# Two feed-forward blocks of a decoder trunk: gate and up by seven half-size block products in place of eight

## The reference, cut to what matters

```python
def rmsnorm(x, g):
    y = x * lax.rsqrt(jnp.mean(x * x, axis=-1, keepdims=True) + EPS)
    return y * g

def swiglu_ffn(h, w_gu, w_down):
    g, u = jnp.split(h @ w_gu, 2, axis=-1)
    return (jax.nn.silu(g) * u) @ w_down

def reference(x, mem, ...):            # x (1, 512, 1024), all float32
    for i in range(2):
        x = x + 0.5 * swiglu_ffn(rmsnorm(x, n_ffn1[i]), ffn1_w_gu[i], ffn1_w_down[i])
        x = x + mixer(rmsnorm(x, n_mix[i]))           # i = 0: gated linear attention, i = 1: pooling
        x = x + mem_cross_attn(rmsnorm(x, n_xattn[i]), rmsnorm(mem, n_mem[i]), ...)
        x = x + 0.5 * swiglu_ffn(rmsnorm(x, n_ffn2[i]), ffn2_w_gu[i], ffn2_w_down[i])
    return rmsnorm(x, n_final)
```

## Time and profile before

| | |
|---|---|
| median of 3 runs | 1993.26 us (1993.07 to 1993.73) |
| span of the profiled execution | 1992.3 us |
| PE busy | 1983.5 us (100%) |
| DVE busy | 930.9 us (47%) |
| ACT busy | 710.2 us (36%) |
| POOL busy | 160.8 us (8%) |
| mean granted TensorE clock | 0.999 of 2.4 GHz |

### The profile page before, as it was taken

The page is one execution under the profiler, slowest core; times in us unless marked ns, Lnnn a source line. Parts: engine busy times, 40 slices in busy tenths (PEclk is TensorE's granted clock), DMA queues, the critical chain, the costliest instruction groups (busy, mean ns, idle before and its releaser), DMA issues.

```text
span 1992.3 us, 23096 instructions
## 1 busy us (share of the span) xinstructions
PE 1983.5 (100%) x9182; PEld 1654.4 (83%) x9182; DVE 930.9 (47%) x1007; ACT 710.2 (36%) x865; POOL 160.8 (8%) x201
## 2 busy tenths in 40 slices
PE   9999999999999999999999999999999999999998
PEld 7888888888898888888888888888898888888887
DVE  5343443487865654434343443433287544434323
ACT  5222232256554543222222322222156443322222
POOL 2000001100112120000001000000112022200000
PEclk9999999999999999999999999999999999999999
DMA  5323352323434533232223323222353324432221
GB/s 176 105 88 102 100 142 76 104 64 106 129 126 127 169 106 106 84 105 88 96 95 100 106 84 105 87 98 95 121 165 114 103 85 127 158 105 96 94 95 74
DMA packets 204153, 214.53 MB, mean 108 GB/s; under 512 B 21970, under 2 KB 186960, under 8 KB 204096
## 3 DMA queue, kind: packets, MB, share of 16 engines
q1 hardware_dynamic: 180416, 192.95, 29.6%
q0 software_dynamic: 6432, 17.64, 3.4%
q10 hardware_dynamic: 17248, 3.16, 0.9%
HBM read 203.23 MB, written 10.49 MB: 107 GB/s over the span
## 4 chain that ended last, share of the span: by engine, by line
PE 96%; DVE 1%; DMA 1%; ACT 1%; issue 1%; SPq 0%; ACTq 0%; POOL 0%; DVEq 0%
PE ps L368 32%; PE ps L369 32%; PE ps L370 32%; DMA p_scratch<-sq 0%; ACT w_hi L1198 0%; DVE w_lo L1731 0%; DMA raw<-in_ffn_w_gu 0%; DVE sums L2213 0%; DMA p_tok<-p_scratch 0%; DVE sums L2233 0%; SPq L390 0%; DVE up L2411 0%; SPq L418 0%; PE ps L943 0%; PE ps L1138 0%
## 5 line engine op out<-in xcount | busy, mean ns | idle before, releaser
L368 PE MATMUL ps<-h_hi,w_hi 128*128 128x512 f32 (+1 forms) x1728 | 667.3, 386 | 0.2 <-DVE h_lo L1734 0.2
L369 PE MATMUL ps<-h_lo,w_hi 128*128 128x512 f32 (+1 forms) x1728 | 665.8, 385 | 0.0
L370 PE MATMUL ps<-h_hi,w_lo 128*128 128x512 f32 (+1 forms) x1728 | 665.8, 385 | 0.0
L1731 DVE TENSOR_TENSOR w_lo<-raw,w_hi 128x2048 fp32r<-128x2048 f32 (+4 forms) x195 | 417.4, 2141 | 461.8 <-ACT w_hi L1198 461.8
L1198 ACT ACTIVATE w_hi<-raw 128x2048 fp32r<-128x2048 f32 (+4 forms) x195 | 347.6, 1783 | 271.0 <-PE ps L370 266.9
L368 PEld LDWEIGHTS ps<-h_hi,w_hi 128*128 128x128 f32 x1728 | 324.7, 188 | 65.8 <-DVE h_lo L1734 0.9
L370 PEld LDWEIGHTS ps<-h_hi,w_lo 128*128 128x128 f32 x1728 | 324.6, 188 | 64.8
L369 PEld LDWEIGHTS ps<-h_lo,w_hi 128*128 128x128 f32 x1728 | 324.7, 188 | 64.0
L368 PE MATMUL ps<-mid_hi,w_hi 128*128 128x512 f32 x528 | 205.6, 389 | 0.0
L370 PE MATMUL ps<-mid_hi,w_lo 128*128 128x512 f32 x528 | 205.5, 389 | 0.0
L369 PE MATMUL ps<-mid_lo,w_hi 128*128 128x512 f32 x528 | 205.5, 389 | 0.0
(11 more groups left out here) (361 smaller groups left out, 1909.2 us busy)
## 6 DMA issues: line engine op xcount, KB each, us to landing
raw<-in_ffn_w_gu SPq DMA_DIRECT2D x87, 1024.0 KB, 5.1
raw<-in_ffn_w_down SPq DMA_DIRECT2D x34, 1024.0 KB, 4.9
raw<-in_x_w_kv SPq DMA_DIRECT2D x16, 1024.0 KB, 5.9
raw<-in_gla_w_in SPq DMA_DIRECT2D x12, 1024.0 KB, 5.1
raw<-in_ffn_w_down SPq DMA_DIRECT2D x12, 768.0 KB, 4.3
raw<-in_x_w_q SPq DMA_DIRECT2D x8, 1024.0 KB, 4.9
raw<-in_x_w_o SPq DMA_DIRECT2D x8, 1024.0 KB, 6.1
raw<-in_gla_w_out SPq DMA_DIRECT2D x8, 512.0 KB, 3.5
```

The costliest lines, as they stand in the source:

```text
L368: nc.tensor.matmul(out_ap, left[0], right[0], start=first, stop=False)
L369: nc.tensor.matmul(out_ap, left[0], right[1], start=False, stop=False)
L370: return nc.tensor.matmul(out_ap, left[1], right[0], start=False, stop=last)
L1731: return nc.vector.tensor_tensor(out_ap, value, hi.bitcast(F32), ALU.subtract)
```

## The change

It touches blocks 1 and 2 only. In each, chunks 0 and 1 ("plain" slots) are computed as before, except that a slot now holds the gate chunk and the up chunk of one index, 128 columns each, loaded by two DMAs of 512 KB. The other 20 chunks of each block ("mixed" slots, 40 in all) treat gate and up of a chunk as a product of 2 x 2 blocks: contraction rows 0 to 3 and 4 to 7, output columns gate and up, tokens 0 to 255 and 256 to 511. Seven block products (P1 to P7, each 4 rows x 3 = 12 matmuls of 128 x 256) replace eight. For it, four sums of weight quarters (`w_sums`) are made per slot, and four sums of token/feature quarters of `x` (`x_sums`, `s_hi`, `s_lo`) per block. A slot's seven stationary forms (4 x 128 x 128 each) are split one by one into eighths of `w_hi` and `w_lo`. P4 of a chunk is computed in the next chunk's slot. Results meet in PSUM: ACT copies P1's bank into another bank, PE adds P6 onto it, DVE adds P5 (parked in `sq` by ACT) and writes a further bank, and PE adds P7, P3 and P4 there.

The gate/up phase is cut in two parts of 11 chunks (the first with the 2 plain ones), each followed by a down phase over its own 11 chunks (slots of 6 and 5 rows, four pairs), so that `mid` takes half the room; the residual is added to `x` twice. PE runs mixed slots in a loop of two; ACT and DVE have them written out.

```diff
+    P1, P5, P6, P4, P2, P7, P3 = range(PRODUCTS)
+    LEADING = (P1, P5, P6, P2)
 ...
+            def block_product(n, m, i, bank):
 ...
+                for kk in range(KH):
+                    right_hi, right_lo = activation_form(i, kk)
+                    to, fresh = ps[:, bank, 0:TH], i in (P1, P5) and kk == 0
+                    nc.tensor.matmul(to, hi[:, kk, :], right_hi, start=fresh, stop=False, skip_group_check=True)
+                    nc.tensor.matmul(to, hi[:, kk, :], right_lo, start=False, stop=False, skip_group_check=True)
+                    last = nc.tensor.matmul(to, lo[:, kk, :], right_hi, start=False, stop=kk == KH - 1,
 ...
+            def last_block(n, part):
 ...
+                pe.wait_ge(sig.mixed_dve_step, dve_step(end - 1, C22_READY))
+                block_product(n, end, P4, banks[(end - 1 - mixed_first[n, part]) % 2])
+
+            def half_down(n, part):
 ...
+                pe.wait_ge(sig.mixed_dve_step, dve_step(end - 1, C12_TAKEN))
 ...
             def ffn(n, between=None):
 ...
+                if n in MIXED:
+                    project(("gu", n, 0), hh, feed=(None, 3, 4, 7)[n])
+                    project(("gu", n, 1), hh)
+                    for part in range(2):
+                        mixed_slot(n, part, 0)
+                        with pe.Fori(0, (mixed_count(n, part) - 1) // 2) as j:
+                            for l in (1, 2):
+                                mixed_slot(n, part, l, j)
+                        last_block(n, part)
+                        half_down(n, part)
```

ACT in a mixed slot (l counts the mixed slots of a part, m those of the kernel; `form_hi` writes one form's high part once PE has done the product that used its place):

```diff
+                    nc.scalar.activation(ps[:, banks[l % 2], 0:TH], ps[:, 6, 0:TH], ACT.Copy).then_inc(sig.mixed_act_step, 1)
+                    if l > 0:
+                        form_hi(m, P3, sig.product_done, product_count(m - 1, P3))
+                    if following:
+                        form_hi(m + 1, P1, sig.product_done, product_count(m, P1))
 ...
+                    hi_part(sq[:, s % 2, TH:], ps[:, 7, 0:TH]).then_inc(sig.mixed_act_step, 1)
```

POOL makes one sum per mixed slot, all four of the first mixed slot of a part:

```diff
+            def third_sums(n, part):
+
+                for m in range(mixed_first[n, part] + 1, mixed_end(n, part)):
+                    w = mixed_slots[m]
+                    pool.wait_ge(raw_loaded[w % 2], loaded[w])
+                    pool.wait_ge(*form_lo_count(m - 1, P7))
+                    third_sum(m)
 ...
             pool.dma_start(mem_cols[1][:], mem_scratch.rearrange("(c p) t -> p c t", p=P)).then_inc(sig.mem_loaded, 16)
+            weight_sums(1, 0)
+            third_sums(1, 0)
```

The sums of x are made between the residuals of the last two pairs before the block (DVE; ACT has the matching high parts):

```diff
+            def feed_last_pairs(f, pair, split_after, residual):
+
+                if pair == 2:
 ...
+                    sum_x(f, 0)
+                    split_next(split_after)
+                    x_sums_lo(f, 0)
+                    sum_x(f, 1)
+                else:
+                    residual(6)
+                    feed(f, 6)
+                    x_sums_lo(f, 1)
+                    residual(7)
+                    feed(f, 7)
+                    sum_x(f, 2)
+                    split_next(split_after)
+                    x_sums_lo(f, 2)
+                    sum_x(f, 3)
+                    sums_lo(f)
+                    x_sums_lo(f, 3)
```

More of the change, by code:

```diff
@@ L75, in place, with place_mixed @@
         if rows:
+            area.append(placed["plain"] % 2)
+            if mixed:
+                mixed_slots.append(len(slot_end))
+            else:
+                placed["plain"] += 1
+            loaded.append(16 * loads + (loaded[-2] if len(loaded) > 1 else 0))
             slot_end.append(placed["parts"])
             slot_rows.append(rows)
+    def place_mixed(n):
+        for part in range(2):
+            for s in range(part * HALF, (part + 1) * HALF):
+                if s < PLAIN_FIRST:
+                    place(("gu", n, s), 2, 2, C, loads=2)
+                else:
+                    if s in (PLAIN_FIRST, HALF):
+                        mixed_first[n, part] = len(mixed_slots)
+                    place(("gu", n, s), 0, 0, C, mixed=True, loads=2)
+            for pair in range(C // 2):
+                for g, (_, rows) in enumerate(HALF_GROUPS):
+                    place(("down", n, part, pair, g), 2, 2 if g == 1 else 0, rows)
     def place_ffn(n):
+        if n in MIXED:
+            place_mixed(n)
+            return
         for s in range(FC):
@@ L414, in load_ffn @@
                 first = 0
+                if n in MIXED:
+                    both = gu[layer].rearrange("(k p) (g n) -> p k g n", p=P, g=2)
+                    for part in range(2):
+                        for s in range(part * HALF, (part + 1) * HALF):
+                            w = at[("gu", n, s)].slot
+                            sp.wait_ge(sig.w_lo_ready, w - 1)
+                            for g in range(2):
+                                sp.dma_start(raw[:, w % 2, :, g * P:(g + 1) * P], both[:, :, g, s * P:(s + 1) * P])\
+                                  .then_inc(raw_loaded[w % 2], 16)
+                        for pair in range(C // 2):
+                            for g, (row, nrows) in enumerate(HALF_GROUPS):
+                                load_fixed(("down", n, part, pair, g), down[layer], part * HALF + row, nrows, pair * COLS)
+                    return
                 if n == 0:
@@ new lines, in mixed_ffn @@
+            def mixed_ffn(n, between):
+                norm_root((None, 3, 4, 7)[n])
+                load_silu()
+                for part in range(2):
+                    mixed_run(n, part)
+                    if part == 1 and between is not None:
+                        between()
+                    if (n, part) == (2, 1):
+                        band_split()
+                    f = FEED_AFTER[n]
+                    for pair in range(C // 2):
+                        split_next(at["down", n, part, pair, 0].slot)
+                        w = at["down", n, part, pair, 1].slot
+                        if part == 1 and n + 1 in MIXED and pair >= 2:
+                            feed_last_pairs(f, pair, w)
+                        elif part == 1:
+                            feed(f, 2 * pair)
+                            feed(f, 2 * pair + 1)
+                            split_next(w)
+                        elif pair < 3:
+                            split_next(w)
@@ L1586, in cross @@
                 for pair in range(4):
+                    if i == 0 and pair >= 2:
+                        feed_last_pairs(3, pair, at[("xo", 0, pair)].slot)
+                        continue
                     for m in (2 * pair, 2 * pair + 1):
@@ new lines, in mixed_ffn, with residual @@
+            def mixed_ffn(n, between):
+                norm_inverse((None, 3, 4, 7)[n])
+                f = FEED_AFTER[n]
+                for part in range(2):
+                    mixed_run(n, part)
+                    if part == 1 and between is not None:
+                        between()
+                    if (n, part) == (2, 1):
+                        band_split()
+                    def residual(m):
+                        name = ("down", n, part, m // 2, 1)
+                        o, c = at[name].out + m % 2, m % 2
+                        bank = part_bank(name, c)
+                        nc.vector.scalar_tensor_tensor(t[:, c, :], ps[:, bank, :], 0.5, rms[:], ALU.mult,
+                                                       ALU.mult).then_inc(sig.evacuated, 1)
+                        dve.wait_ge(sig.evacuated, o + 1)
+                        if part == 1:
+                            dve.wait_ge(sig.x_half_ready, OPENED + C * MIXED.index(n) + m + 1)
+                        nc.vector.tensor_tensor(x[:, m, :], x[:, m, :], t[:, c, :], ALU.add)\
+                          .then_inc(sig.x_ready if part == 1 else sig.x_half_ready, 1)
+                        if (n, part) == (2, 1) and m >= 4:
+                            dve.wait_ge(*x_final(5, m))
+                            nc.vector.transpose(xg_blocks[:, m - 4, :], x[:, m, :]).then_inc(sig.x_blocks_ready, 1)
+                    for pair in range(C // 2):
+                        split_next(at["down", n, part, pair, 0].slot)
+                        w = at["down", n, part, pair, 1].slot
+                        if part == 1 and n + 1 in MIXED and pair >= 2:
+                            feed_last_pairs(f, pair, w, residual)
+                            continue
+                        for m in (2 * pair, 2 * pair + 1):
+                            residual(m)
+                            if part == 1:
+                                feed(f, m)
+                        if part == 1 or pair < 3:
+                            split_next(w)
@@ L1748, in part @@
                 return (at[name].out + c) % 4
+            part_bank = part
             def feed(f, m):
```

494 lines of the change are left out of this document (460 added, 34 removed).

## The result

| | before | after |
|---|---|---|
| median | 1993.32 us (12 runs) | 1997.61 us (12 runs) |
| span of the profiled execution | 1992.3 us | 1996.1 us |
| mean granted TensorE clock | 0.999 | 0.994 |

The ratio is 1.0017, with a 95% interval of 1.0009 to 1.0025. The changed kernel is 0.2% slower: 4.3 us by the medians, 3.4 by the ratio, about what I said could just be told from no change. The forecast of 1983.1 was 14.5 us too low, 14.0 of them in the span. One of the 12 runs after the change took 2419.95 us, at a mean granted clock of 0.752, and is left out of the ratio.

What follows compares the result with a forecast made beforehand. PE was taken as the bound, busy 1983.5 of 1992.3 us. -32.3 + 4.1 + (6.0 + 2.9) + (6.2 + 2.9) = -10.2 gave a span of 1982.1 and a median of 1983.1 us, range 1972 to 2003.

Steps and rivals of the forecast that it cites:

- (b): Norm of blocks 1 and 2: PE waits for acc_parts, 6.0 us in block 1 and 6.2 in block 2.
- (c): From the norm to the first seed: PE stands at the first P6 and P7, 2.9 us in both blocks.
- half clock: PE's clock behind stalls: no term in the forecast, 0 us.
- the pooling band: Slot behind the pooling band in block 2: no term in the forecast, 0 us.
- the second parts: Start of a block's second gate/up part: forms ready in time, 0 us of stall.
- the gain: Mixed slots: 84 short matmuls take 10.08 us against 10.88; 32.3 us less over 40 slots.
- POOL's lock in block 1: At block 1's norm, POOL's two adds and three weight sums delay DVE 0.7 us each on average, 3.6 us.
- DVE has 0.9 us over, 0 us of stall: Mixed slots: DVE has 0.9 us spare, 0.6 after POOL's sum, so PE stalls 0 us per slot.
- The loads: Mixed slots' loads in 512-byte rows: 0 us. Rival: late load, 1993.9 us, chance 0.12 shared with PE's sequencer falling behind.
- (a): Four down-phase starts: PE waits for the low part and the fourth bank, 1.0 us each, 4.1 in all.
- DVE doesn't pace the slots: Denies the rival that DVE's order paces the mixed slots: 2004.7 us, slower than before; chance 0.18 for 2000 or more.
- PE's sequencer keeps up: Denies the rival that register instructions and waits stall PE in mixed slots: about 1994 us; chance 0.12 shared with late loads.

Runs made afterwards that it cites:

- third_dve: Changed kernel with the third weight sum of the 36 following mixed slots made by DVE instead of POOL: 1994.72 us.
- down_start: Changed kernel with the starts of the four down phases rearranged: ACT's next high part earlier, DVE's half part last, PE's fourth-bank wait later: 1994.07 us.
- pool_late: Changed kernel with POOL's four weight sums of a block's first mixed slot waiting for the low part of the acc sums: 1992.65 us.
- norm_early: Changed kernel with the acc split before blocks 1 and 2 moved right behind the third x sum, in ACT and DVE: 2000.58 us.
- both: Changed kernel with POOL's four first-slot weight sums waiting for acc's low part, and the acc split moved ahead of the next slot's split: 1999.92 us.
- heads: Changed kernel with ACT, DVE and POOL work reordered at the starts of blocks 1 and 2, several edits at once: 1985.37 us.
- band_late: Changed kernel with the pooling band's split moved from ahead of block 2's last down phase to behind its first pair: 1993.07 us.
- pe_unrolled: Changed kernel with PE's loop over pairs of mixed slots written out, constants replacing a register for the waits: 1997.15 us.

## Why the prediction was wrong

The span came out 14.0 us above the sum. The two starts, (b), (c) and the half clock between them taken together, took 22.1 us for the 18.0 forecast, 4.1 more. The slot behind the pooling band took 4.5 with its half clock, for 0; the second parts 2.1, for 0; the down phases 0.9 more than forecast; 0.3 is the gain, and 2.1 is not attributed. The steps that failed are the zeros for the band, for the second parts and for the clock, and the size of POOL's lock in block 1. The median adds 0.5, since it lies 1.5 us above the profiled span here and not 1.0. The part of an execution around its own span is neither: it is 1.7 to 1.8 us in every execution of the kernel before that the experiments list, and 2.0 to 2.1 in those of the changed one.

**The gain (right).** 0.120 us a matmul, 10.08 a slot. The "0.806 unrounded" doesn't follow from the rows: 21.76 / 2 - 10.08 is 0.80, and the gain 32.0.

**DVE has 0.9 us over, 0 us of stall (right, for a reason I had only half).** The period and DVE's idle place are as worked out. That the lock feeds back on itself, 0.09 us a slot, I didn't see; `third_dve` shows that even 0.6 us more of DVE work stalls nothing.

**The loads (right).** The 512 KB DMAs land after 4.9 us, and no slot waits for one.

**(a) 1.0 us four times (right, 1.24).** `down_start` showed it to be the waits named.

**(b) "At 0.7 on average": the norm (mechanism right, too small in block 1).** The term that was mis-sized is the lock: I took 3.6 us for all five of POOL's operations, each costing DVE a share of its length, as where the two take turns in rows 8. `pool_late` took 4.3 us off block 1's stall and 3.1 off block 2's. In block 2 they do take turns, and its 6.4 us is near my 6.2. In block 1 three sums back to back cost DVE 4.3 us in one piece. What `pool_late` leaves, 3.3 and 3.1 us, is also more than the 2.4 and 2.6 that I had worked out for DVE's own work. And where I expected POOL's sums to be stretched to 1.8 to 2.3 us, they took 1.27 to 1.48: DVE did the waiting.

**(c) The first seed, 2.9 (found 1.4, and not a term of its own).** It and the norm are one chain; `norm_early` and `both` moved the time from one to the other. In `heads`, where ACT's copy comes earlier among other changes, the stall at P6 is gone; that ACT's order alone made it late is not shown.

**"Nothing there" for the second parts (wrong, 2.1).** I worked out the forms and left out POOL's first following sum, which starts with P7's low part just ahead of DVE's column sum: 1.78 us instead of 0.68.

**The band (wrong, 2.8, and 1.7 of half clock behind it).** The step that failed is one that I didn't make: I costed what the change moves at the down phases, not what stood there already with less in store behind it. `band_late` gives the 4.5 us back.

**Half clock (wrong).** I priced a stall at its length. 6.8 us were lost to half clock behind three stalls, but the 5.1 behind the two norms are not all extra: block 1's came off the wait at P6, and block 2's held up the chain by 0.86 us. So in this kernel it cost 1.7 us behind the band and, as an estimate from that wait, up to 0.9 more.

Of the rivals none came about. DVE doesn't pace the slots, no load is late, and PE's sequencer keeps up (`pe_unrolled`). The chance that I gave to "slower" hung on the first of these, and slower came from the pauses between the stretches that I had studied. That the time lies inside the range of 1972 to 2003 is luck: its upper end was meant for slots that lose over 0.55 us, and they lost nothing. The chance of "faster" was also added up wrongly: 0.50 x 0.97 + 0.20 + 0.015 is 0.70, not 0.72.

The Trainium skill (SBUF — State Buffer, "SBUF: two separate sides") has the lock held for the whole instruction, and the other engine fully blocked. Block 2's rows agree: each of DVE's sums lost 0.9 to 1.1 us beside a POOL sum of 1.47 or 1.48. The 4.74 us in block 1 go beyond: DVE's one sum ended behind three of POOL's in a row, of 3.8 us together. By the rule alone it would have lost up to 1.3 us there.

What stays open: why DVE got no turn between POOL's sums in block 1 and did in block 2, why a pause sometimes costs half clock and sometimes not, and the 2.1 us that the table gives as rest.

## What to carry to other kernels

A change that wins a little in each of many steady slots is decided at their ends: for every phase start, follow the chain from the last thing that both kernels share to the first steady slot, and price it as one chain. A wait that was hidden before is hidden only as long as the store in front of PE is as large as before; count that store again when tiles get smaller. And GpSimd sums beside VectorE ones are dear where VectorE is on the chain: three in a row cost it 4.3 us here, more than their own 3.8. Look for a place where they cost nothing, as beside the reciprocal.

## What the hardware showed

- Three POOL sums of 1.3 us issued back to back kept a VectorE sum of 0.42 us going for 4.74, beyond the third; in the next block, with the same six instructions, the engines took turns, and three VectorE sums took 1.40 to 1.51. Moved into the 3.35 us of DVE's reciprocal (one input, one output) in `heads`, POOL's sums took 1.28 each and the reciprocal its 3.35.
- A pause of TensorE can cost more than itself. Behind idle times of 7.6 and 6.25 us its matmuls had double distance, at a granted clock of 0.50, for 5.3 and 5.6 us: 2.5 and 2.6 us lost. Idle times of 2.19 to 2.93 us occur at 16 places of these traces; behind 13 of them 1.3 to 2.8 us were lost and behind 3 almost nothing. In `heads` 2.88 us of idle time cost 1.29 in block 1 and 0.1 in block 2. Behind the many of 0.9 to 1.1 us that stood alone it was never more than 0.4.
- Half clock costs nothing more where TensorE would have had to wait anyway: in block 1 the 2.5 us lost to it came off the next wait.
